# Two 512 x 1024 blocks on one core: in the FFN gate blocks the second weight sum is made on VectorE, not by an accumulating DMA

## The reference, cut to what matters

```
def swiglu(h, w_gate, w_up, w_down):
    return (jax.nn.silu(h @ w_gate) * (h @ w_up)) @ w_down

for layer in range(DEPTH):                      # DEPTH = 2
    x = x + 0.5 * swiglu(rmsnorm(x, norm_ffn1[layer]), ffn1_gate[layer], ffn1_up[layer], ffn1_down[layer])
    x = x + hybrid_mixer(rmsnorm(x, norm_mix[layer]), ...)
    x = x + 0.5 * swiglu(rmsnorm(x, norm_ffn2[layer]), ffn2_gate[layer], ffn2_up[layer], ffn2_down[layer])
```

## Time and profile before

| | |
|---|---|
| time, median of 3 runs | 3652.09 us (3649.52 to 3656.58) |
| the profiled execution | 3649.27 us, span 3647.4 us |
| granted TensorE clock, mean | 0.994 |
| TensorE busy | 3543.2 us, 97% of the span |
| VectorE busy | 2513.1 us, 69% |
| ScalarE busy | 1804.8 us, 49% |
| GpSimd busy | 285.7 us, 8% |
| DMA, SyncE's queue | 303.97 MB, 23.0% of 16 engines |
| DMA, GpSimd's queue | 167.78 MB, 21.0% |

### The profile page before, as it was taken

The page is one execution under the profiler, slowest core; times in us unless marked ns, Lnnn a source line. Parts: engine busy times, 40 slices in busy tenths (PEclk is TensorE's granted clock), DMA queues, the critical chain, the costliest instruction groups (busy, mean ns, idle before and its releaser), DMA issues.

```text
span 3647.4 us, 53611 instructions
## 1 busy us (share of the span) xinstructions
PE 3543.2 (97%) x20848; PEld 3028.1 (83%) x20848; DVE 2513.1 (69%) x3210; ACT 1804.8 (49%) x2527; POOL 285.7 (8%) x317
## 2 busy tenths in 40 slices
PE   9999899999999999999999999999999999999999
PEld 7776688888678887989977798999998977789988
DVE  4455666666755767787767577887888676578885
ACT  3335344436633444655555456555655554546554
POOL 0001000000200000100000220000000000310000
PEclk9999999999999999999999999999999999999999
DMA  4000256422005663577621016776777421017774
GB/s 185 36 35 35 92 162 183 140 105 93 24 35 173 173 174 117 172 199 221 176 87 57 12 53 172 201 217 179 204 204 194 133 106 50 2 63 210 207 197 132
DMA packets 70668, 475.18 MB, mean 130 GB/s; under 512 B 7952, under 2 KB 8336, under 8 KB 17552
## 3 DMA queue, kind: packets, MB, share of 16 engines
q1 hardware_dynamic: 46224, 303.97, 23.0%
q0 software_dynamic: 24192, 167.78, 21.0%
HBM read 404.62 MB, written 2.10 MB: 112 GB/s over the span
## 4 chain that ended last, share of the span: by engine, by line
PE 75%; DVE 16%; ACT 5%; DMA 2%; issue 2%; DVEq 0%; POOL 0%; ACTq 0%; SPq 0%; POOLq 0%
PE ps L670 73%; DVE split L2531 6%; ACT arena L1479 3%; DVE arena L2531 3%; PE ps L679 2%; DVE X L2535 2%; ACT split L1479 2%; DMA ring<-in_wts 2%; DVE arena L2535 2%; ACT L1479 1%; DVE arena L3629 0%; DVE ring L2531 0%; DVE small L2547 0%; DVE arena L2527 0%; DVE arena L2559 0%
## 5 line engine op out<-in xcount | busy, mean ns | idle before, releaser
L670 PE MATMUL ps<-split 128*128 128x512 f32 (+1 forms) x16236 | 2955.3, 341 | 51.2 <-DVE arena L2531 14.1
L670 PEld LDWEIGHTS ps<-split 128*128 128x128 f32 x16236 | 2506.9, 191 | 419.3 <-issue 60.3
L2531 DVE TENSOR_TENSOR split<-ring,split 128x1024 fp32r<-128x1024 f32 x674 | 823.0, 1221 | 422.7 <-ACT split L1479 372.6
L1479 ACT ACTIVATE split<-ring 128x1024 fp32r<-128x1024 f32 x674 | 709.7, 1053 | 720.9 <-PE ps L670 660.4
L1479 ACT ACTIVATE arena<-ps 128x512 f32<-128x512 f32 (+5 forms) x656 | 343.0, 523 | 377.1 <-PE ps L670 258.3
L670 PE MATMUL ps<-arena 128*128 128x128 f32 (+9 forms) x3344 | 485.5, 297 | 23.2 <-ACT arena L1479 8.8
L670 PEld LDWEIGHTS ps<-arena 128*128 128x128 f32 (+2 forms) x3344 | 393.8, 190 | 98.0 <-issue 65.6
L1479 ACT ACTIVATE split<-arena 128x1024 fp32r<-128x1024 f32 (+2 forms) x242 | 251.8, 1040 | 211.6 <-PE ps L670 131.4
L2531 DVE TENSOR_TENSOR split<-arena,split 128x1024 fp32r<-128x1024 f32 (+2 forms) x242 | 290.2, 1199 | 79.6 <-ACT split L1479 60.1
L2531 DVE TENSOR_TENSOR arena<-arena 128x512 f32<-128x512 f32 (+7 forms) x302 | 215.2, 713 | 32.7 <-ACT arena L1479 15.7
L2535 DVE SCALAR_TENSOR_TENSOR X<-ps,X 128x512 f32<-128x512 f32 x252 | 174.4, 692 | 69.0 <-PE ps L670 47.5
(11 more groups left out here) (114 smaller groups left out, 1214.2 us busy)
## 6 DMA issues: line engine op xcount, KB each, us to landing
ring<-in_wts SPq DMA_DIRECT2D x260, 1024.0 KB, 5.4
arena<-in_wts POOLq DMA_DIRECT2D x80, 1024.0 KB, 8.4
ring<-ring POOLq DMA_DIRECT2D x28, 1024.0 KB, 9.5
ring<-arena POOLq DMA_DIRECT2D x24, 1024.0 KB, 7.7
ring<-in_wts SPq DMA_DIRECT2D x41, 512.0 KB, 3.5
ring<-in_wts POOLq DMA_DIRECT2D x14, 1024.0 KB, 8.0
arena<-arena POOLq DMA_DIRECT2D x6, 1024.0 KB, 10.3
arena<-in_wts POOLq DMA_DIRECT2D x8, 512.0 KB, 4.5
```

Source lines behind the costliest of these rows:

```text
L670: return e.matmul(out, l, r, start=start, stop=stop, skip_group_check=True)
L1479: o.sig(a.activation(out, i, f, **kw), sig)
L2531: o.sig(v.tensor_tensor(out, a, b, op), sig)
```

## The change

T2 of a gate block is now made by VectorE: `second(U, q)` adds piece q of T1 (b12's slot) and b22 and writes it to b11's slot, semaphore `f_two`. It is called after each T1 piece's split in a wide block (r = 1), once at r = 1 in a narrow block, and twice at r = 2 in the first block. The GpSimd transfers that made T2 in gate blocks are gone (`opened` and line 3916 for them); down blocks keep theirs. T4's transfer waits for `f_two` where it waited for `f_t2`. The next loads into b12's and b22's slots wait for `f_two` too. In the first block, the third `next(extra)` (F6's form) moves out of `first(U)` to the beginning of step r = 3, which on ScalarE is behind the copy of N5; on VectorE the low part of F5 is made before the sum for F6.

```diff
+            downs += 16 * (not B.gated)
+            for pc in next(of for (what, _, _), of in zip(B.order, B.of) if what == "P6"):
+                seconds += B.gated
+                pc.sum = ("f_two", seconds) if B.gated else ("f_t2", downs)
+            B.two = pc.sum
...
+            if B.gated:
+                B.loads["b12"].added = B.loads["b22"].added = B.two
...  # ScalarE, first(U)
             split(next(below))
-            next(extra)
             split(next(below))
...  # ScalarE, gate_up, after the early copies of step r
+                if U.first and r > 2:
+                    next(extra, None)
...  # VectorE
+    def second(U, q):
+
+        r = {b: K.RING[:, ld.slot, :] for b, ld in U.loads.items()}
+        v.wait_ge(S[f"ring{U.loads['b22'].slot}"], U.loads["b22"].landed)
+        p = U.of[2][q]
+        c = slice(p.q * U.w, (p.q + p.c) * U.w)
+        tt(r["b11"][:, c], r["b12"][:, c], r["b22"][:, c], ALU.add, "f_two")
...  # VectorE, whole()
+                    lo("f5", F.shape, 1)
                     tt(F.sixth, F.shape, F.a11, ALU.subtract, "h_sum")
-                    lo("f5", F.shape, 1)
...  # VectorE, first(U)
             split(next(below))
             split(next(below))
-            next(extra)
...  # VectorE, gate_up
                 if r == 2:
                     two(U)
+                    if U.first:
+                        second(U, 0)
+                        second(U, 1)
+                if r == 1 and not wide:
+                    second(U, 0)
+                if U.first and r > 2:
+                    next(extra, None)
...
+                    if r == 1 and wide:
+                        second(U, y)
...  # GpSimd, block(U)
-        if U.first:
-            g.wait_ge(S["f_two"], begun)
-            g.dma_start(at["b11"], b22, accum_op=ALU.add).then_inc(S["f_t2"], 16)
-            g.wait_ge(S["used"], U.begin)
-            ...
-        else:
-            g.wait_ge(S["lo"], U.before.split["t3"])
-            ...
+        g.wait_ge(*((S["used"], U.begin) if U.first else (S["lo"], U.before.split["t3"])))
+        g.dma_start(t3, b22).then_inc(S["f_base"], 16)
+        g.wait_ge(S["f_base"], U.count)
+        g.dma_start(t3, b12, accum_op=ALU.add).then_inc(S["f_t3"], 16)
+        if not U.gated:
             g.wait_ge(S["lo"], U.split["b11"])
             g.wait_ge(S["f_t1"], U.of[2][-1].sum[1])
             g.wait_ge(S["f_t3"], U.count)
             g.dma_start(at["b11"], t3, accum_op=ALU.add).then_inc(S["f_t2"], 16)
         g.wait_ge(S["lo"], U.split["b21"])
-        g.wait_ge(S["f_t2"], U.count)
+        g.wait_ge(S[U.two[0]], U.two[1])
         g.dma_start(at["b21"], at["b11"], accum_op=ALU.add).then_inc(S["f_t4"], 16)
...  # GpSimd, where opened(...) was called before a stage's blocks
-        if j == 1:
-            opened(lins["ffn10"][0])
-        if l:
-            opened(lins["ffn11"][0])
-        opened(lins[f"ffn2{l}"][0])
```

More of the change, by code:

```diff
@@ L245, in plan @@
     lins, loads, turned, forms, n = {}, [], [], [], 0
-    sums, shapes, before, blocks, summed_up, done, holds = 0, 0, None, 0, 0, 0, {}
+    sums, shapes, before, blocks, summed_up, seconds, downs, done, holds = 0, 0, None, 0, 0, 0, 0, 0, {}
     slots, held, kept = [0, 1, 2, 3], {}, {}
@@ L373, in ffn @@
     def ffn(l, n_):
-        nonlocal n, blocks, summed_up, shapes, done
+        nonlocal n, blocks, summed_up, seconds, downs, shapes, done
         key, new, us = f"fgu{n_}_{l}", [], []
@@ L405, in block @@
         def block(name, key, p, h, kbase, c1, c2, w, at=None):
-            nonlocal blocks, summed_up
+            nonlocal blocks, summed_up, seconds, downs
             blocks += 1
@@ L3882, in pool_program @@
     Y, M = K.y, K.m
[L3885 to L3894, removed]
+    F = K.f
     def block(U):
@@ L3900, in block @@
         t3 = (F.t3first if U.first else F.t3)[:, 0:n]
-        if U.first:
-            g.wait_ge(S["f_two"], begun)
-            g.dma_start(at["b11"], b22, accum_op=ALU.add).then_inc(S["f_t2"], 16)
-            g.wait_ge(S["used"], U.begin)
-            g.dma_start(t3, b22).then_inc(S["f_base"], 16)
-            g.wait_ge(S["f_base"], U.count)
-            g.dma_start(t3, b12, accum_op=ALU.add).then_inc(S["f_t3"], 16)
-        else:
-            g.wait_ge(S["lo"], U.before.split["t3"])
-            g.dma_start(t3, b22).then_inc(S["f_base"], 16)
-            g.wait_ge(S["f_base"], U.count)
-            g.dma_start(t3, b12, accum_op=ALU.add).then_inc(S["f_t3"], 16)
+        g.wait_ge(*((S["used"], U.begin) if U.first else (S["lo"], U.before.split["t3"])))
[3 more added lines that the diff above has]
+        if not U.gated:
             g.wait_ge(S["lo"], U.split["b11"])
```

## The result

The changed kernel took 3675.11 us (median of 4 runs, 3668.84 to 3679.35) beside 3651.49 us for the kernel before: 1.0061 times as long, 95% interval 1.0043 to 1.0079. It is slower by 22 us in the means and 23.6 us in the medians. The forecast was 3661.5, +9.4 us, with a range of 3646 to 3672: the sign was right, the size less than half of what came. The profiled execution took 3668.84 us with a span of 3667.0, which is 19.6 us more than the span before. It is the fastest of the four; what follows accounts for these 19.6 us.

The account below looks back on a forecast made before the run. TensorE, busy in 97% of the span, was taken as the bound, the cost hanging on where VectorE's queue is full. Terms +9.1, +8.5 and -8.2 gave +9.4 us on 3652.1, so 3661.5 us, range 3646 to 3672.

Parts of the forecast that it names:

- VectorE's load: All four FFN stages: 44 adds of 128x1024 on VectorE at 1226 ns each, 53.9 us more busy time.
- the two bounds, 0 and 53.9: Cost of the adds: 0 us if all fall in VectorE's idle time, 53.9 us if all are on the path.
- First block, order and P6: First blocks: N3 starts earlier, but P6 waits 3.2 us for T2's first piece in VectorE's full queue; sum +9.1 us.
- N3 ahead of down blocks: Eight gate blocks ahead of a down block: adds delay b22's first piece, about 1 us gap before N3; +8.5 us.
- Relief of the loads: Before N4 ahead of down blocks: earlier T4 transfer frees b12's load, 3.0 us gaps go; -8.2 us in sum.
- T4 in the first blocks: First blocks: b12's and b11's loads go out beside T4's transfer at about 1520, wanted 14 us later; priced at 0.
- bunched transfers: Rival, first blocks: T4's transfer and two loads start together, b22 lands late, +12 to +20 us; bunched or no relief 0.15.
- T4 in the narrow blocks: Four narrow blocks: VectorE's 1.88 us wait for T2 covers the add of 1.3 us; nothing, otherwise 5 us.
- the three terms that I priced: First blocks +9.1, N3 in eight blocks ahead of a down block +8.5, load relief -8.2; sum +9.4 us.
- the two that I set to nothing: First blocks' loads beside T4's transfer, and the adds in the four narrow blocks: each predicted at 0.

Follow-up runs that it names:

- e1: Kernel before with only the first block's new order, T2 still made by DMAs everywhere; ratio to the kernel before 0.9994.
- e2: Kernel before with the new first-block order and T2 added on VectorE in the four first blocks only; ratio to the kernel before 1.0047.
- e3: Kernel before with the new first-block order and T2 added on VectorE in the sixteen later wide blocks only; ratio to the kernel before 1.0013.
- e6: Changed kernel with T4's transfer of later wide blocks held back until b22's first piece is split; ratio to the kernel before 1.0141.
- e4: Changed kernel, but in first and narrow blocks the next load into b12's slot waits until T4's transfer lands; ratio to the kernel before 1.0067.
- e10: e8 with T4's transfer issued in two halves, each as soon as its add is done; ratio to the kernel before 1.0034.
- e13: e11 without the VectorE adds: T2 by DMA everywhere, same order, later forms and halves; ratio to the kernel before 0.9980.
- e8: Changed kernel with A11's form and its difference moved behind b22's pieces in blocks ahead of a down block; ratio to the kernel before 1.0084.
- e11: e3 with the form work one step later and T4's transfer in two halves; ratio to the kernel before 0.9973.

## Why the prediction was wrong

*VectorE's load.* Right: 44 adds, 53.1 us more. The time came out between the two bounds, 0 and 53.9, and far from both.

*First block, order and P6.* Right in mechanism and place, 10.2 for 9.1, with P6 waiting 3.3 us for 3.2. T2's first piece ended 0.5 us later than worked out. N3 never waited for ScalarE in stage one; at most 0.8 us was foretold. The 0.81 us before N5's second piece, where VectorE's two sums stand ahead of it, I had not listed. P6 must wait for the end of that queue anyway, so a gap ahead of P6 mostly takes its length from P6's.

*N3 ahead of down blocks.* Right: eight gaps of 1.12 us, 9.0 for 8.5.

*Relief of the loads.* Right in size: the gaps of 3.0 us became 0.65, 0.29 and none, the waits of the T1 adds went from 12.7 to 2.0 us, the 0.84 us shows in all eight down blocks; -7.3 for -8.2. The mechanism, an earlier T4 transfer, carries only part of it. With the order alone (e1), where T4's transfer still waits for T2's, these places are already at 11.1 in place of 14.9 (11.7 in e2, which has the same order), and the waits of the T1 adds at 7.4 us; e3, with the adds in these blocks, has 7.8 and 1.8 us. So about half of the relief came with the order, which I had not priced here, and why was not looked into. The other thing I did not see is how narrow the relief stands: with a T4 transfer held back (e6) it is gone.

*T4 in the first blocks: the step that failed.* I wrote that b12's and b11's loads go out with T4's transfer at about 1520 and "I price it at 0 and put its end into the range". The margin I gave was that of the loads. What was late was the transfer in that same bundle, which I had not followed to its reader. Before, the two DMAs had T2 ready so early that T4's transfer left at 1513.62. Now it waits for VectorE's second add at 1520.68, left at 1521.24 and, beside two loads, landed 14.5 us later, as the transfer before had done in 15.1. Its 7.6 us of lateness ate the slack in front of N4 and 4.7 us over the four stages came out. e4 and e10 each took them away. The rival that I called bunched transfers had the place (three transfers together at 1520) and the wrong victim: b22's load. Its "over 11 us each" does not fit either; the first of the two loads took 5.9 us.

*T4 in the narrow blocks: the same failure.* "Covers the add of 1.3: nothing" holds for T2's split. But VectorE got to the add at 1794.58, T4's transfer left at 1796.37 in place of 1791.04, and, 0.5 MB of it, landed in 8.35 us beside a load issued at 1795.88; before it had taken 6.39. +3.6 us. Where the narrow blocks keep the DMA (e2, e3), their gap is 0.87 us as before. In both places the DMA made T2 sooner than VectorE came to it; taking a transfer off a queue is no gain for what hangs on it if the engine that takes over is behind.

*The clock.* It does not explain the 19.6 us between the profiled executions. Five gaps before (of 1.77 to 3.03 us) and four after (of 2.48 to 3.34) were followed by some us at the lower clock; behind the 2.00 us gap of the earlier trace rows and two of the changed kernel's four gaps before P6 it stayed at 1.00. The windows of the kernel before, ahead of and behind the 3.03 us gap of the earlier trace rows, and of the changed kernel behind the 2.60:

```profile
1570.00:1575.00 5.00, 4.92 (x41) 4.64 (x39) 4.44 (x5) 0.73 (x2) 0.55 (x1) 1.00 0.85 288
1578.20:1583.70 5.50, 5.50 (x26) 5.50 (x27) 4.73 (x5) 3.20 (x5) 0.26 (x1) 0.50 0.87 164
```

```profile
1539.00:1545.00 6.00, 5.97 (x37) 6.00 (x38) 5.29 (x6) 3.23 (x4) 0.43 (x1) 0.72 1.02 218
```

At 0.50, which is 1.2 GHz, 26 matmuls took 5.50 us; at full speed that is 3.2 us by the 48 in 5.85. The sums of the two kernels differ by about one such stretch. The clock may bear on the 4 us by which the medians differ more: the changed kernel's profiled execution had a mean granted clock of 0.996, the other three 0.992 to 0.993 and 6.0 to 10.5 us more. The kernel before shows the same from run to run: 3640.86 us at 0.997 and 3657.68 at 0.992, beside e13.

Together: the three terms that I priced came to 10.2 + 9.0 - 7.3 = 11.9 in place of 9.4, and the two that I set to nothing to 4.7 + 3.6 = 8.3. That is 20.2 in place of 9.4, and three quarters of the 10.8 us missed are T4's transfer.

## What to carry to other kernels

When work moves from a DMA to an engine, follow the thing made, not only the engine: when is it ready, which transfer or load does that release, beside what does it then run, and who reads it. A transfer whose waits show nowhere in the profile can be the slack of a product some steps on. Before closing a gap of an engine, look for what it hides: e8's 9.0 us came back as 10.1, and only with the next wait moved as well did the time fall. And run the control without the change's main idea, as e13 did here; the gain came without it.

## What the hardware showed that was not expected

- One accumulating transfer of 1 MB within on-chip memory landed in 6.9 us alone, 12.0 us beside one load of 1 MB and part of another, and 14.5 us beside two; the loads beside it took 5.9 and 12.6 us where their median is 5.4 to 5.7.
- A gap of TensorE can cost more than its length. Behind 4.5 us of waiting 24 matmuls ran at a granted clock of 0.53 and took 5.33 us, some 2.4 us over. Behind the 3.34 us gap of e10's first block 96 matmuls took 13.23 us, and 11.74 behind the same gap in the changed kernel. There the clock stayed at 1.00 until the next gap of 2.60, and then fell. e11 has no gap over 1.04 us in the four stages, and its windows behind P6 and N4 of the first blocks show 1.00.
- Two halves of 512 KB that overlap took 4.8 and 10.1 us from issue to landing beside two loads; the whole took 13.0 in e8. Cutting the transfer cost nothing that the gaps show, and let its first half start 2.4 us ahead of the second.
